# Turning the prompt's memory keys in 32-blocks on VectorE instead of on TensorE, with a shared token order

## What is computed

```
hm   = rmsnorm(mem_prompt)                       # 256 tokens x 2048
mk   = hm @ w_ck ; mv = hm @ w_cv                # both also outputs, as they stand
scores[h] = qx[h] @ mk[:, h].T * 512**-0.5       # 512 x 256
probs     = softmax(scores over the 256 tokens)
ctx[h]    = probs @ mv[:, h]
```

## Time and profile before

| what | value |
|---|---|
| runs (3) | 1666.84 to 1667.59 us, median 1667.03 us |
| span of the profiled execution, first to last instruction | 1663.2 us, 3.8 us under the median of the runs |
| TensorE busy | 1643.0 us (99%) |
| VectorE, ScalarE, GpSimd busy | 969.9, 673.3, 183.7 us |
| DMA | 229.79 MB, 138 GB/s over the span |
| granted TensorE clock | 0.998 of 2.4 GHz over the span |

### The profile page before, as it was taken

How to read it: one execution, slowest core, us unless ns; L and a number is a source line. 1 busy time by engine, 2 the same in 40 slices (tenths; PEclk the granted TensorE clock), 3 DMA queues, 4 the chain that set the end, 5 groups by cost and what they waited for, 6 DMA issues and landing times.

```text
span 1663.2 us, 31696 instructions
## 1 busy us (share of the span) xinstructions
PE 1643.0 (99%) x12906; PEld 1522.8 (92%) x12906; DVE 969.9 (58%) x1676; ACT 673.3 (40%) x1146; POOL 183.7 (11%) x191
## 2 busy tenths in 40 slices
PE   7999999999999999999999999999999999999998
PEld 5887899999999999999999999999999987499998
DVE  5776446665756647565433343333887753499952
ACT  5566345254442543435322222222343333344542
POOL 0121001111121112111100001111000000001120
PEclk9999999999999999999999999999999999999999
DMA  7898734243232432333333334444223399733462
GB/s 266 261 295 254 219 92 119 55 109 99 70 99 53 115 91 77 91 84 96 101 81 83 86 104 139 132 132 138 62 87 97 98 388 396 229 103 105 126 187 108
DMA packets 277534, 229.79 MB, mean 138 GB/s; under 512 B 10825, under 2 KB 244178, under 8 KB 271970
## 3 DMA queue, kind: packets, MB, share of 16 engines
q1 hardware_dynamic: 277184, 228.42, 44.9%
q10 hardware_dynamic: 258, 0.09, 0.0%
HBM read 201.31 MB, written 27.53 MB: 138 GB/s over the span
## 4 chain that ended last, share of the span: by engine, by line
PE 92%; DVE 4%; issue 1%; ACT 1%; DMA 1%; POOL 0%; SPq 0%; DVEq 0%; ACTq 0%; POOLq 0%
PE pj L287 48%; PE pj L486 10%; PE pj L2203 7%; PE dk L2203 5%; PE pj L2946 2%; PE dk L2515 2%; PE pj L2539 1%; PE dk L2439 1%; PE dk L1819 1%; PE pj L2450 1%; PE pj L2548 1%; PE dk L1272 1%; PE dk L1278 1%; PE dk L825 1%; PE dk L2975 1%
## 5 line engine op out<-in xcount | busy, mean ns | idle before, releaser
L287 PE MATMUL pj<-a_hi,w_high 128*128 128x272 f32 x1792 | 394.1, 301 | 0.0
L287 PE MATMUL pj<-a_hi,w_low 128*128 128x272 f32 x1792 | 370.4, 288 | 0.0
L287 PE MATMUL pj<-a_lo,w_high 128*128 128x272 f32 x1792 | 369.7, 288 | 0.0
L287 PEld LDWEIGHTS pj<-a_hi,w_high 128*128 128x128 f32 x1792 | 280.9, 189 | 13.4 <-issue 8.1
L271 DVE TENSOR_TENSOR w_low<-w_raw,w_high 128x2048 fp32r<-128x2048 f32 x76 | 173.9, 2288 | 192.7 <-ACT w_high L261 192.6
L287 PEld LDWEIGHTS pj<-a_lo,w_high 128*128 128x128 f32 x1792 | 281.6, 189 | 0.0
L287 PEld LDWEIGHTS pj<-a_hi,w_low 128*128 128x128 f32 x1792 | 280.1, 189 | 0.1
L261 ACT ACTIVATE w_high<-w_raw 128x2048 fp32r<-128x2048 f32 x76 | 145.4, 1913 | 57.9 <-PE pj L287 45.9
L2087 ACT ACTIVATE q_high<-q_part 128x512 fp32r<-128x512 f32 x140 | 77.5, 620 | 73.3 <-DVE q_part L2141 37.0
L287 PE MATMUL pj<-mix_hi,w_high 128*128 128x272 f32 x512 | 105.9, 288 | 0.0
L287 PE MATMUL pj<-mix_lo,w_high 128*128 128x272 f32 x512 | 105.5, 288 | 0.0
(11 more groups left out here) (482 smaller groups left out, 3029.5 us busy)
## 6 DMA issues: line engine op xcount, KB each, us to landing
w_raw<-in_w_in_dram SPq DMA_DIRECT2D x48, 1024.0 KB, 5.9
w_raw_wide<-in_w_ck_dram SPq DMA_DIRECT2D x16, 1024.0 KB, 8.6
w_raw_wide<-in_w_cv_dram SPq DMA_DIRECT2D x16, 1024.0 KB, 7.9
w_raw<-in_w_out_dram SPq DMA_DIRECT2D x16, 1024.0 KB, 6.0
q_part<-in_w_cq_dram SPq DMA_DIRECT2D x48, 256.0 KB, 3.6
w_raw<-in_w_co_dram SPq DMA_DIRECT2D x8, 1024.0 KB, 8.3
q_part<-in_w_co_dram SPq DMA_DIRECT2D x32, 256.0 KB, 3.8
xr<-xT_scratch SPq DMA_DIRECT2D x16, 272.0 KB, 6.3
```

The costliest lines, as they stand in the source:

```text
L287: mm = pe.matmul(pj[:, 2 * (q % 2) + b, 0:n], wt[:, k, :], x(k, o, n), start=(k == 0 and m == 0), stop=(k == KT - 1 and m == 2))
```

## The change

The keys are turned on VectorE, which turns each 32x32 block by itself. `kts` holds, on partition `32*i + r`, column `r` of every 32-block of columns for the 32 tokens of quadrant `i`, for both halves `m` of 128 tokens. It is stored by four DMAs, one for each quadrant of partitions, in runs of 64 values (256 bytes), and the scratch has the tokens in the order quadrant, half, token of 32. The values of the prompt are loaded in the same order by four DMAs a head in place of one. TensorE's turns and ScalarE's copies of the keys go, with semaphore `m_turned`.

```diff
-        kts = take("kts", [4, MEM])
+        kts = take("kts", [4 * P // T32, 2, T32])
...
                         sp.wait_ge(kts_ready, 2 * j)
-                        sp.dma_start(kT_d[4 * j - 4:4 * j, :, :].rearrange("k p r -> p k r"), kts[:]).then_inc(kts_stored, 16)
+                        for i in range(4):
+                            dst = kT_d[4 * j - 4:4 * j, :, i * 2 * T32:(i + 1) * 2 * T32].rearrange("k (b p) r -> p (k b) r", p=T32)
+                            sp.dma_start(dst, kts[i * T32:(i + 1) * T32].rearrange("p n m r -> p n (m r)")).then_inc(kts_stored, 16)
...
-            def turn_keys(g, i):
...
-                    if 1 <= j <= KEY_GROUPS and 1 <= q <= 2:
-                        steps[6] = [turn_keys(j - 1, q - 1)]
...
             if 0 < g <= KEY_GROUPS:
-                eng.wait_ge(m_turned, 2 * g)
+                eng.wait_ge(kts_ready, 2 * g)
...
-                    if 1 <= j <= KEY_GROUPS and 1 <= q <= 2:
-                        g, i = j - 1, q - 1
-                        act.wait_ge(m_turned, 2 * g + i + 1)
-                        at_least(act, kts_stored, 16 * g)
-                        act.activation(kts[:, 2 * i:2 * i + 2, :].rearrange("p d m -> p (d m)"), dk[:, 3, :], ACT.Copy).then_inc(kts_ready, 1)
...
+                    if 1 <= j <= KEY_GROUPS and 1 <= q <= 2:
+                        dve.wait_ge(pj_read, 4 * j)
+                        at_least(dve, kts_stored, 64 * (j - 1))
+                        dve.transpose(kts[:, :, q - 1, :], mst[:, q - 1, :].rearrange("p (n d) -> p n d", d=T32)).then_inc(kts_ready, 1)
...
         def sp_vtb(sp, h):
-            sp.dma_start(vtb[h % 2][:], t["mem_v_prompt"][0, 0, :, h, :].rearrange("(m p) d -> p m d", p=P)).then_inc(vtb_loaded[h % 2], 16)
+            for i in range(4):
+                src = t["mem_v_prompt"][0, 0, :, h, :].rearrange("(m i r) d -> i m r d", i=4, r=T32)
+                sp.dma_start(vtb[h % 2][(i % 2) * 2 * T32:(i % 2 + 1) * 2 * T32, i // 2, :], src[i]).then_inc(vtb_loaded[h % 2], 16)
...
-                    pe.wait_ge(vtb_loaded[h % 2], 16 * (h // 2) + 16)
+                    pe.wait_ge(vtb_loaded[h % 2], 64 * (h // 2) + 64)
```

More of the change, by code:

```diff
@@ L329, in build @@
         x_bank = sem("x_bank")
-        xts_stored, kts_stored, m_turned, kts_ready, mst_stored = (sem(n) for n in (
-            "xts_stored", "kts_stored", "m_turned", "kts_ready", "mst_stored"))
+        xts_stored, kts_stored, kts_ready, mst_stored = (sem(n) for n in (
+            "xts_stored", "kts_stored", "kts_ready", "mst_stored"))
         mem1_loaded = sem("mem1_loaded")
@@ L2218, in sp_cq @@
             sp.wait_ge(sums_done, 1)
-            sp.wait_ge(kts_stored, 64)
+            sp.wait_ge(kts_stored, 256)
             sp.wait_ge(mst_stored, 128)
@@ L2755, in sp_co @@
             sp.wait_ge(y_stored[1], 32)
-            for s, v in ((mst_stored, 128), (kts_stored, 64), (xts_stored, 80), (st_stored, 768), (s_stored, 128),
+            for s, v in ((mst_stored, 128), (kts_stored, 256), (xts_stored, 80), (st_stored, 768), (s_stored, 128),
                          (s0_stored, 128), (ust_stored, 16 * 72), (old_rows, 16), (x2_stored[0], 128), (x2_stored[1], 128)):
```

## The result

The changed kernel takes 1695.68 us (median of 5 runs, 1694.46 to 1696.67) against 1667.03 (5 runs, 1665.93 to 1667.59) for the kernel before on the same chip. The ratio is 1.0172, with a 95% interval of 1.0159 to 1.0184: slower by 28.7 us, where 18.4 was forecast. It lies in the forecast range and, at 1695.7, at the far end of the likeliest case's own (1678 to 1697).

The account below looks back on a forecast made before the run. TensorE, busy 1643.0 of 1663.2 us, was taken to bound the kernel. Memory stage -2.0 and attention stage +20.4 gave +18.4 on 1667.0, so 1685.4 us, with a range from 1664 to 1700.

Parts of the forecast that it names:

- likeliest case: Values' loads in the attention stage run on two engines, 16 to 30 us slower, 1678 to 1697; chance 0.60.
- memory stage: Over four key groups, TensorE's removed turns gain 2.0 us of at most 3.5, the rest lost to waiting.
- first place, landings: Attention stage, value loads of heads 0 and 1: `ktb` of head 2 lands late, TensorE waits 11.6 us.
- second place, landing: Attention stage, value loads of heads 2 and 3: request 7's values land late, TensorE waits 8.8 us.
- the rate of an engine: Values' loads: 24.9 GB/s an engine, so a head takes 10.5 us on two engines against 1.3 on 16.
- Of 0.88 us a group some 0.5 to 0.6 is left: Memory stage, each key group: TensorE comes 0.88 us sooner but waits 0.3 us for ScalarE's cast.
- wait for TensorE anyway: Memory stage, quarter 1: VectorE's transpose stands ahead of copies to `xts` that wait for TensorE in any case.
- Two engines that share a way into SBUF: Values' loads at half the rate, 21 us a head: 1727, or toward 1700 if not in step; chance 0.20.
- All engines: Values' loads use all 16 engines and cost nothing: 1665, between 1663.5 and 1667; chance 0.16.
- The memory stage loses: Longer store and VectorE's transposes hold the casts in all four groups: 1667 to 1670 with 16-engine loads; chance 0.04.
- the 9.4 to 12.6 that bounded them: Memory stage, keys' store: lands between the old store's 9.4 us and the `xts` store's 12.6, at most 3.2 later.

Follow-up runs that it names:

- e1: Kernel before with only the changed value loads, four DMAs a head with the two halves outermost: 1697.99 us, ratio 1.0184.
- e3: Changed kernel with 32 tokens outermost in the value loads' source, the two halves side by side in `kts`: 1666.7 us, ratio 0.9998.
- e7: Kernel before with four value loads a head whose source has four pieces of 16 tokens outermost: 1673.61 us, ratio 1.0041.
- e8: Kernel before with the changed value loads for heads 2 and 3 alone: 1680.88 us, ratio 1.0083.
- e6: Changed kernel with eight value loads a head, each VectorE transpose replaced by a copy of one column: 1664.08 us, ratio 0.9986.
- e9: Changed kernel with eight value loads a head, VectorE's copy into `mst` moved behind its copies into `xts`: 1664.14 us, ratio 0.9983.
- e10: Changed kernel with eight value loads a head, transposes moved behind copies others wait for, `mst` copy behind the `xts` copies: 1662.3 us, ratio 0.9972.
- e2: Changed kernel with the old value loads, one DMA a head: 1665.91 us, ratio 0.9996.
- e11: Kernel before with only its copy into `mst` moved behind the copies into `xts`: 1666.17 us, ratio 0.9999.

## Why the prediction was right, and where it was off

**The place and the cause were right.** Slower, by value loads on two engines, which delay `ktb` of head 2 and the values of request 7: e1 has the whole loss, e3 takes it away by the outermost index alone, and e7 has the step between.

**The size was 10.3 us too small: 28.7 against 18.4.** The terms:

| term | forecast us | measured us |
|---|---|---|
| memory stage | -2.0 | 0 |
| first place, landings | +11.6 | +14.3 (5.1 + 1.4 + 7.8) |
| second place, landing | +8.8 | +11.1 |
| lower clock behind the waits | none | +4.5 (2.7 + 1.8) |

The measured terms add up to 29.9, against 31.7 between the spans; 0.5 of the rest is there before the first copy into `mst`, and the remaining 1.3 us, 1.1 of it behind the attention stage (201.9 us against 200.8), was not traced. The scatter between executions is of that size: e8's span is 202.8 us long there, with the same work.

*Landings.* The mis-sized term is the rate of an engine, 24.9 GB/s in all circumstances. It holds while two engines move alone. Beside the requests' values the same loads complete 3.0 to 4.1 us apart in place of 2.6, and `ktb` of head 2 is delayed by 21.5 us, not 18.4. The trace has it in the single packets: alone, one of 2 KB takes 85 ns (median), against 84 before the change; from 1389 to 1402 us it takes 133, and one of 8 KB of the requests' values 467 in place of 309. In the kernel before the two kinds run side by side (1377 to 1379.5 us) at 84 and 309. So the slowing is mutual, and these runs have it only where a load fills 64 partitions or 32 and not 128; what on the way causes it was not isolated.

*The clock.* The prediction has no term for it. It treats a wait as costing its own length, but after the 7.8 us wait TensorE works for 5 us at 1.2 GHz, and the other two waits do the like: 2.7 us on scores(2), 1.8 on request 7. The 1.4 us on request 0 are inside the wait for `ktb` and cost nothing more.

*The memory stage.* The step that failed is "Of 0.88 us a group some 0.5 to 0.6 is left". The transpose at 0.70, `rbc` later, and the 0.3 us wait for ScalarE's cast are all as written; the cast costs 0.2 us a group. But the forecast followed the later `rbc` to the cast alone, and of the copies to `xts` it looked only at those of quarter 1, which "wait for TensorE anyway", not at those of the next group's quarter 0. The same delay goes on through `a_hi` and `a_lo` to VectorE, and the shortened TensorE meets it at a second point, at the start of quarter 1, with about 0.1 us of cover in the trace of before. That costs 0.9 us a group. In e6, without a transpose, the order of the copies still takes half of the gain; in e9, with the order mended, the transposes take about as much; e10 has all of it.

**The rivals.** *Two engines that share a way into SBUF:* fell. Alone, the two engines move 50 GB/s, not 25, though they fill partitions 32 apart. The Trainium skill has these on one port ("SBUF — State Buffer", "Door 1: The DMA port swizzle"); the trace shows no loss from it at two engines, whose 2 KB packets take 85 ns against 84 before. Whether a shared way has a part in the longer packets beside the requests' values, no run here can tell. *All engines:* fell, by the 50 GB/s and by e7. *The memory stage loses:* it doesn't, by e2; the last of a group's four stores has landed 7.8 to 9.5 us after the first was issued, at or under the lower end of the 9.4 to 12.6 that bounded them.

## What to carry to other kernels

Read the outermost index of a DMA's source before its size: with 2 there, a load of 128 KB held two engines for 2.6 us, and 1 MB of such loads delayed the load of `ktb` behind them by 21.5 us; the same bytes with 32 tokens outermost delayed it by 3.8.

When work is taken from the engine that sets the time, look for the slack at every point where it meets another engine, not only at the next one: here the gain of 3.5 us was used up at two points of 0.2 and 0.9 us a group, and came through only when both were cleared. Follow a delay to the end of its loop, past the first engine that waits for it. And count a long wait of TensorE with the slow matmuls behind it, here 4.5 us on 24 us of waits.

## What the runs showed that was not expected

After waits of 5.1, 7.8 and 11.1 us TensorE started at 1.2 GHz, and the matmuls of the values took 3.34 and 3.64 us in place of 1.85 to 1.93. TensorE was still at that level 5 us into its scores.

The stores of `kts` in 256 B runs, four times as many packets for the same 512 KB, had all landed 7.8 to 9.5 us after the first issue, where the one store in 1 KB runs took 8.0 to 9.7. The smaller packets cost nothing that showed.

The taking away of 32 turns of 0.11 us gave 4.0 us in the stage in place of 3.5. The kernel before loses most of the other 0.5 us at the second meeting point itself: on its chain three sets of four turns (at 73.33, 98.27 and 123.28 us) take 0.53 to 0.59 us and the others before 140 us 0.44, together 0.38 us. In e11, with the copy moved, all of them take 0.44, and the stage takes 169.6 us.
